# A transformer pair on one core: all q and k products of the attention ahead of v, heads one by one

## What is computed

```python
qkv = (y @ w_qkv[i]).reshape(B, S, 3, N_HEADS, HEAD_DIM)      # 16 heads of 64
...
s_own = jnp.einsum('bhqd,bhqkd->bhqk', qi, k_own) * scale
s_own = s_own + rel_bias[:, rel_bucket(qpos[:, None] - kpos_own[None, :])]
s_own = jnp.where(kpos_own[None, :] <= qpos[:, None], s_own, NEG)
p = jax.nn.softmax(...)
out = jnp.einsum('bhqk,bhkd->bhqd', p, v_own)
...
h = h + o.transpose(0, 2, 1, 3).reshape(B, S, D) @ w_o[i]
```

## Time and profile before

| | |
|---|---|
| median of 3 runs | 975.1 us (972.58 to 975.62) |
| profiled execution | 974.01 us, its span 972.2 us |
| TensorE busy | 926.5 us (95%), 7996 matmuls |
| VectorE busy | 667.2 us (69%) |
| ScalarE busy | 504.9 us (52%) |
| GpSimd busy | 65.2 us (7%) |
| DMA | 177.31 MB, mean 182 GB/s |
| attention's stretch | from 646.93 us (first tile of q2 0) to 765.48 us (end of wo2 3) |

### The profile page before, as it was taken

One profiled execution on the slowest core, in us unless ns is written; L12 is line 12 of the kernel. 1 busy time (PEld: TensorE's weight loads), 2 busy tenths in 40 slices (PEclk: granted clock), 3 DMA queues, 4 the chain that ended last, 5 costly groups with the idle time before them and its releaser, 6 DMA issues.

```text
span 972.2 us, 18558 instructions
## 1 busy us (share of the span) xinstructions
PE 926.5 (95%) x7996; PEld 880.7 (91%) x7996; DVE 667.2 (69%) x1113; ACT 504.9 (52%) x821; POOL 65.2 (7%) x91
## 2 busy tenths in 40 slices
PE   5789999999999999999989999989999999999997
PEld 2588888898899999989989999979998999999997
DVE  3876677557579986778758875465656677777643
ACT  2476666544344556455334444465565566665442
POOL 0100012011000000030000001010000300000001
PEclk9799999999999999999999999999999999999999
DMA  8743222232249985446898775515343345555631
GB/s 321 265 157 127 88 88 91 85 131 88 88 158 359 351 299 219 174 179 253 253 290 318 265 241 186 197 43 197 131 140 108 107 177 196 186 174 166 235 120 44
DMA packets 27681, 177.31 MB, mean 182 GB/s; under 512 B 2864, under 2 KB 5680, under 8 KB 7504
## 3 DMA queue, kind: packets, MB, share of 16 engines
q1 hardware_dynamic: 27600, 176.13, 51.5%
HBM read 174.29 MB, written 1.84 MB: 181 GB/s over the span
## 4 chain that ended last, share of the span: by engine, by line
PE 71%; DVE 12%; ACT 7%; DMA 7%; issue 2%; SPq 0%; DVEq 0%; ACTq 0%
PE ps L1002 38%; PE ps L1008 19%; DVE wl L1696 3%; DMA raw<-in_w_fi_dram 3%; DVE acc L1631 2%; ACT wh L1343 2%; PE ps L1000 2%; DMA raw<-in_ada_dram 1%; DMA raw<-in_w_rest_dram 1%; DVE tmp L1658 1%; PE ps L1046 1%; DMA raw<-in_w_sc_dram 1%; PE ps L1140 1%; PE ps L1054 1%; PE ps L1201 1%
## 5 line engine op out<-in xcount | busy, mean ns | idle before, releaser
L1002 PE MATMUL ps<-HH,wh 128*128 128x256 f32 x1480 | 388.0, 294 | 6.4 <-DVE wl L1696 5.5
L1696 DVE TENSOR_TENSOR wl<-raw,wh 128x1024 fp32r<-128x1024 f32 x265 | 321.4, 1233 | 97.2 <-ACT wh L1343 96.5
L1002 PE MATMUL ps<-HH,wl 128*128 128x256 f32 x1480 | 375.2, 285 | 0.0
L1343 ACT ACTIVATE wh<-raw 128x1024 fp32r<-128x1024 f32 x265 | 272.6, 1040 | 171.8 <-PE ps L1008 105.3
L1002 PEld LDWEIGHTS ps<-HH,wh 128*128 128x128 f32 x1480 | 287.1, 194 | 15.8 <-issue 8.0
L1002 PEld LDWEIGHTS ps<-HH,wl 128*128 128x128 f32 x1480 | 287.1, 194 | 2.1 <-issue 2.1
L1008 PE MATMUL ps<-HL,wh 128*128 128x256 f32 x1480 | 241.5, 286 | 2.6 <-DVE HL L1671 2.2
L1008 PEld LDWEIGHTS ps<-HL,wh 128*128 128x128 f32 x1480 | 207.3, 194 | 3.3 <-DVE HL L1671 2.6
L1002 PE MATMUL ps<-FH,wl 128*128 128x256 f32 x352 | 88.8, 285 | 0.0
L1002 PE MATMUL ps<-FH,wh 128*128 128x256 f32 x352 | 88.1, 279 | 0.0
L1631 DVE SCALAR_TENSOR_TENSOR acc<-raw,silc,acc 128x512 f32<-128x512 f32 x101 | 76.6, 758 | 8.4 <-DMA raw<-in_ada_dram 5.2
(11 more groups left out here) (251 smaller groups left out, 1090.1 us busy)
## 6 DMA issues: line engine op xcount, KB each, us to landing
raw<-in_ada_dram SPq DMA_DIRECT2D x32, 1024.0 KB, 5.3
raw<-in_w_fi_dram SPq DMA_DIRECT2D x22, 1024.0 KB, 4.9
raw<-in_w_up_dram SPq DMA_DIRECT2D x22, 1024.0 KB, 4.8
raw<-in_w_rest_dram SPq DMA_DIRECT2D x20, 1024.0 KB, 4.8
raw<-in_w_in_dram SPq DMA_DIRECT2D x16, 1024.0 KB, 4.8
raw<-in_w_qkv_dram SPq DMA_DIRECT2D x12, 1024.0 KB, 4.8
raw<-in_w_o_dram SPq DMA_DIRECT2D x8, 1024.0 KB, 4.7
raw<-in_w_fo_dram SPq DMA_DIRECT2D x8, 1024.0 KB, 4.9
```

The costliest lines, as they stand in the source:

```text
L1002: e.matmul(o, w[:, k, 128 * t:128 * t + 128], x_hi[:, k0 + k, :], start=first and n + k == 0, **MM)
L1343: e.activation(whl[u % HALF][0][:, 0:n], raw[i % RAW][:, c:c + n], ACT.Copy).then_inc(*a_hi.up(u))
L1696: e.tensor_tensor(wl[:, 0:n], raw[i % RAW][:, c:c + n], wh[:, 0:n].bitcast(F32), ALU.subtract).then_inc(*v_lo.up(u))
```

## The change

- The product list is q2 0, k2 0, q2 1, k2 1, q2 2, k2 2, q2 3, k2 3, then v2 0 to 3.
- A head's task begins h % 4 ticks late. It takes a bank for steps 0 to 4 and gives it back when the transposed weights are copied; for steps 5 to 7 it takes a bank again, the first that is free, once v2 j is made. The extra tick behind a late v2 is gone.
- There are 16 buffers apt in place of 4. QA and KA share their place in SBUF with OHh and OLl.
- wo2 0 and wo2 1 are made in turns: unit 0 of both, then unit 1 of both, then both are closed. While they run, weights are split up to four units beyond the first unit of wo2 0, and no further. A second way, high_first, is written and not used.

```diff
-    QA = sb("QA", [128, 8, T], where=phase)
-    KA = sb("KA", [128, 8, T], where=phase)
-    VA = sb("VA", [128, 2, 1024], where=phase)
+    scores = ExitStack()
+    QA = sb("QA", [128, 8, T], where=scores)
+    KA = sb("KA", [128, 8, T], where=scores)
+    scores.close()
     OH = sb("OHh", [128, 8, T], F32R, where=phase)
     OL = sb("OLl", [128, 8, T], F32R, where=phase)
-    heads = [dict(p=sb(f"ap{i}", [128, 384], where=phase), pt=sb(f"apt{i}", [128, 3, 128], where=phase),
-                  st=sb(f"ast{i}", [128, 8], where=phase), bank=psum[4 + i]) for i in range(4)]
+    VA = sb("VA", [128, 2, 1024], where=phase)
+    PT = [sb(f"apt{i}", [128, 3, 128], where=phase) for i in range(16)]
+    heads = [dict(p=sb(f"ap{i}", [128, 384], where=phase), st=sb(f"ast{i}", [128, 8], where=phase), bank=psum[4 + i])
+             for i in range(4)]
...
-    for kind, j in (("q2", 0), ("k2", 0), ("q2", 1), ("k2", 1), ("v2", 0), ("q2", 2), ("k2", 2), ("v2", 1), ("q2", 3),
-                    ("k2", 3), ("v2", 2), ("v2", 3)):
+    for kind, j in [(kind, j) for j in range(4) for kind in ("q2", "k2")] + [("v2", j) for j in range(4)]:
...
     def attend(h):
+
+        for _ in range(h % 4):
+            yield
         while not open_heads:
             yield
         st, before_attend[h] = open_heads.pop(0)
         for k in range(5):
             emit("att", h, k, st)
+            if k < 4:
+                yield
+        open_heads.append((st, (a_att, ("pt", h))))
+        while ("v2", h // 4) not in made or not open_heads:
             yield
-        if ("v2", h // 4) not in made:
-            while ("v2", h // 4) not in made:
-                yield
-            yield
+        st, before_sum[h] = open_heads.pop(0)
         for k in range(5, 8):
             emit("att", h, k, st)
             if k < 7:
                 yield
-        open_heads.append((st, h))
+        open_heads.append((st, (v_att, ("lo", h))))
         made.add(("oa", h))
...
+    def in_turns(ps):
+
+        last = ps[0]["units"][0] + HALF - 1
+        for n in range(2):
+            for p in ps:
+                run_unit(p, n, last)
+        for p in ps:
+            close_product(p)
...
+    together = {("wo2", 0): (in_turns, ("wo2", 1))}
...
         if k == 0:
             a_ev.wait_ge(e, "plain", named["q2", j]["p"])
             a_ev.wait_ge(e, "plain", named["k2", j]["p"])
-            if before_attend[h] is not None:
-                v_att.wait_ge(e, "lo", before_attend[h])
+            free(e, before_attend[h])
...
         elif k == 5:
             a_ev.wait_ge(e, "plain", named["v2", j]["p"])
             a_att.wait_ge(e, "pt", h)
+            free(e, before_sum[h])
```

More of the change, by code:

```diff
@@ L588, in _program @@
     open_streams = [(st, None) for st in range(STREAMS)]
-    before_head, before_attend = {}, {}
+    before_head, before_attend, before_sum = {}, {}, {}
     def gdn(h):
@@ L769, in after @@
                 drain()
-                misc.give(4, v_att, "lo", dict(open_heads)[0])
+                misc.give(4, *[f[0:1] + f[1] for st, f in open_heads if st == 0][0])
             close(n, p)
@@ L814, in operands_of, with open_banks, run_unit, close_product @@
         return [("parts", src, kt // 2) for kt in kts]
[L816 to L820, removed]
+    def open_banks(p):
+        count = 2 if p["split"] else 1
+        while len(main.order) < count:
+            assert tasks
+            tick()
+        taken = [main.take() for _ in range(count)]
+        p["banks"] = [b for b, _ in taken]
+        p["free"] = [f for _, f in taken]
+    def run_unit(p, n, last=None, part=None):
+        u = p["units"][n]
+        if part != "low":
+            split_up_to(u + HALF - 1 if last is None else last)
             low_of(u)
             if n == 0:
[L823 to L829, removed]
-            until(*operands_of(p, units[u]))
[L831 to L835, removed]
+                open_banks(p)
+            until(*operands_of(p, units[u]))
+        tiles = p["width"] // 128
+        for t in range(tiles):
+            emit("mm", u, t, part)
+            if part == "high" or (n, t) != (len(p["units"]) - 1, tiles - 1):
+                tick()
+    def close_product(p):
         after(p)
         tick()
+    def in_turns(ps):
[5 more added lines that the diff above has]
+            close_product(p)
+    def high_first(ps):
+        last = ps[0]["units"][0] + HALF - 1
+        for p in ps:
+            for n in range(2):
+                run_unit(p, n, last, "high")
+        for p in ps:
+            for n in range(2):
+                run_unit(p, n, last, "low")
+            close_product(p)
+    together = {("wo2", 0): (in_turns, ("wo2", 1))}
     def startup():
@@ L870, in _program @@
     for p in products:
-        run(p)
+        if p["kind"] == "proj" and p["j"] == 0:
+            drain()
+        key = p["kind"], p["j"]
+        if key in together:
+            way, second = together[key]
+            way([p, named[second]])
+        elif key not in [second for _, second in together.values()]:
+            for n in range(len(p["units"])):
+                run_unit(p, n)
+            close_product(p)
     drain()
@@ L980, in sync_engine, with pe_product @@
         d_out.wait_ge(e, "out")
-    def pe_product(e, u, t):
+    def pe_product(e, u, t, part):
         un = units[u]
@@ L991, in pe_product @@
         first = un["at"] == 0 and (p["split"] or t == 0)
-        if first:
+        if first and part != "low":
             free(e, p["free"][b])
         v_lo.wait_ge(e, u)
-        for k in range(kn):
+        for k in range(kn) if part != "low" else ():
             high_of(e, src, k0 + k)
@@ L1002, in pe_product @@
                     e.matmul(o, w[:, k, 128 * t:128 * t + 128], x_hi[:, k0 + k, :], start=first and n + k == 0, **MM)
-        for k in range(kn):
+        for k in range(kn) if part != "high" else ():
             low_part(e, src, k0 + k)
@@ L1008, in pe_product @@
                 ins = e.matmul(o, wh[:, k, 128 * t:128 * t + 128], x_lo[:, k0 + k, :], start=False, **MM)
-        ins.then_inc(*p_mm.up(u, t))
+        if part != "high":
+            ins.then_inc(*p_mm.up(u, t))
     def pe_gdn(e, h, k, st):
@@ L1112, in pe_attend @@
             a_att.wait_ge(e, "pt", h)
+            free(e, before_sum[h])
             vs = slice(64 * h, 64 * h + 64)
-            e.matmul(bank[rows, 0:256], VA[:, 0, vs], A["pt"][:, 0:2, :].rearrange("p a b -> p (a b)"), start=True, **MM)
-            e.matmul(bank[rows, 128:256], VA[:, 1, vs], A["pt"][:, 2, :], start=False, **MM).then_inc(*p_att.up("av", h))
+            e.matmul(bank[rows, 0:256], VA[:, 0, vs], PT[h][:, 0:2, :].rearrange("p a b -> p (a b)"), start=True, **MM)
+            e.matmul(bank[rows, 128:256], VA[:, 1, vs], PT[h][:, 2, :], start=False, **MM).then_inc(*p_att.up("av", h))
     def warm(e, n, b, before):
@@ L1300, in act_attend @@
             p_att.wait_ge(e, "turn", h)
-            e.activation(A["pt"][:, :, :].rearrange("p a b -> p (a b)"), b[:, 0:384], ACT.Copy).then_inc(
+            e.activation(PT[h][:, :, :].rearrange("p a b -> p (a b)"), b[:, 0:384], ACT.Copy).then_inc(
                 *a_att.up("pt", h))
```

## The result

The changed kernel took 987.5 us (median of 4 runs, 981.6 to 990.7) beside 974.7 for the kernel before: 1.0144 of its time, interval 1.0105 to 1.0182. Forecast were 985.7, in a range of 979 to 990: the direction is right and the median 1.8 us off. The profiled execution took 989.2 us, its span 987.4 against 972.2.

The account below looks back on a forecast made before the run. TensorE's queue was taken to bound the kernel. Scores +8.5, waits +2.5, transposes -4.4, values +1.6 and their waits +2.5 made +10.6 us unrounded, 974.0 to 984.6 profiled, a forecast median of 985.7, range 979 to 990.

Parts of the forecast that it names:

- Scores: Attention scores on TensorE: 16 lone heads at 0.98 us, 15.7, against four groups at 1.80, 7.2; +8.5 us.
- Waits ahead of scores: Each group's first head directly behind its k product waits for ScalarE's KA copy: three new waits of 0.82, +2.5 us.
- Transposes: Transposes of the softmax weights on TensorE: 16 x 0.33 = 5.3 us with no wait, against 9.7 before; -4.4 us.
- 4. and 5. Values: Weights times V: lone heads, pairs and fours cost +1.6 us; three waits for VA copies behind v products, +2.5.
- part 6: Output products 0 and 1 in turns, later weight splits held back: covered, at nothing; without that cover 1 to 2 us.
- slower still: Rival: transposes wait as before (+3.4 us) or late weight splits are uncovered (+1 to 2): 987 to 991; chance 0.07.
- Sixteen buffers and the shared place: Buffers for transposed weights, and QA and KA sharing space with OH and OL: no instruction more, nothing on a queue.
- the hidden switch: Rival: 0.23 us of each half-array switch is covered, giving 982.2, or 979.7 if half the waits go; chance 0.14.
- the missing lone price: Rival: a lone head costs its quarter of a group; waits stand against transposes, +0.5, 975.6 us; chance 0.07.
- The faster case: Rival: lone heads cost less than their quarter, the neighbouring product's fill or drain hiding in the other half; 971.5; chance 0.04.

Follow-up runs that it names:

- e11: Changed kernel with heads four together, one tile ahead of first readers, output products one after the other, and heads within a group ordered 0, 2, 1, 3: ratio 1.0016.
- e2: Changed kernel with heads beginning in pairs, the second pair one tick later (h % 4 // 2 ticks): 978.4 us, 1.0035 of the kernel before.
- e1: Changed kernel with output products 0 and 1 made one after the other instead of in turns: 983.0 us, 1.0099 of the kernel before.
- e5: Changed kernel, turns kept, but weights split further ahead during the four half products as buffers come free: 1.0093 of the kernel before's time.
- e4: Kernel before with one edit, heads 0 to 11 beginning h % 4 ticks late so their scores stand alone: 1.0048 of the kernel before's time.
- e6: Changed kernel with one tile let pass ahead of each first reader of a k or v product: 980.4 us, 1.0076 of the kernel before.
- e7: Changed kernel with no head beginning late, four heads side by side directly behind their k product: 975.2 us, 1.0018 of the kernel before.

## Why the prediction was right

1. Scores: a lone head was priced at 0.98 us and took 1.04. The sum of the part, forecast +8.5, is 16 x 1.04 - 4 x 1.80 = +9.4. Both halves of the price stand: streaming alone costs 0.65 more (e11), and a pair costs what a lone head costs (e2). The rest, 1.04 - 0.65 = 0.39, is put down to the switch (forecast 0.33). No run has it by itself: a second pair adds 1.80 - 1.05 = 0.75 to a first, and with that for the streaming it would be 0.29. The Trainium skill's rule that a change of mode drains the array (TensorEngine Tiling (Array Packing), Key Properties) agrees in kind, as each piece costs more than its streaming. The estimate of 0.11 us, worked out in the prediction from a figure of the Trainium skill (TensorE: Matmul & The Clock Gate, Step-by-step), is too small against these 0.29 to 0.39.
2. Waits ahead of scores: one of 0.82, which was there before, and three new ones of 0.78. Forecast 0.82 each. Right.
3. Transposes: 16 x 0.33, no wait. Forecast -4.4, measured the same.
4. and 5. Values: pieces of 0.94 (1.27 less the transposes beside them), 1.00 a pair, 1.69 a group, waits of 0.76. Forecast +4.1, measured: 11.5 - 3 x 0.33 - 6.8 = +3.7.
6. **The step that failed** is part 6, the splits held back: "Covered, at nothing". I counted from the moment when wo2 1 ends, with four units to be split and the first needed 2.88 us later. That is right for ScalarE's high parts. But VectorE's list runs one unit behind ScalarE's: the low part of a unit is put in the list when the next unit's high part is. So five low parts were open (the x5 of VectorE's row), and the first was needed at once. VectorE had the 0.69 us of an add and 1.23 of a low part to do between the end of wo2 1 and the start of wo2 2: 1.92, just the wait in the row. With what it cost the tile around it (2.17 in all) and the low clock (1.5), 3.7 us. The price that I had named for a lost cover, in the sum's part 6 and in the case "slower still", was 1 to 2. Either way of queueing the splits in time (e1, e5) takes the stall away.
7. Sixteen buffers and the shared place: nothing was expected of them, and no wait in TensorE's list names them.

The sum of the pieces, forecast 35.1, is 35.5. With the stall (2.2) and the low clock (1.5) that makes 11.0 + 2.2 + 1.5 = 14.7, against a stretch 14.5 longer.

So the sum of +10.6 was 3.9 us short of the stretch's 14.5 and 3.4 short of the ratio's 14.0, and almost all of that is part 6. That the forecast median came out within 1.8 us (985.7 for 987.5) is in part luck: the medians are only 12.9 us apart, where the ratio has 14.0, the four runs reach over 9 us, and the repetition of the same program has 990.3, just above the range. Of the rivals, the hidden switch and the missing lone price are refuted by the 1.04 of a lone head, in the change and in e4, and by e2 and e11. Of "slower still", the half with the late splits came true, at about twice its price; the half with the waiting transposes did not. The faster case named the right lever, but its mechanism is not there: the transposes' 4.4 us are won in the change and in the runs that keep its order and its lone heads (e1, e5, e6), and the lone heads lose twice that.

## What to carry over

Small pieces put between large ones are not free to be scattered. Here two half-array matmul groups on different halves cost as much as one when they stood side by side (1.05 us against 1.04), and each piece paid some 0.3 to 0.4 us on top of its streaming: look for a group's price, and then for a lone one's, before a schedule spreads a group. When a consumer moves directly behind its producer, count the copy between them for each group, and leave one tile for it; here that took away seven waits of 0.77 us. And when a step of a planner is held back, write out the queue of each engine up to the first thing needed; a list that lags by one turns a cover of 2.9 us into none.

## What was not expected of the hardware

Two float32 heads on different halves took 0.87 us from their first matmul to the next product matmul, one alone 0.85. TensorE's granted clock fell to 0.50 in a stretch behind an idle 1.92 us in one execution of the change (and of e2, e6 and e7), and stayed 1.00 there in another execution of the change's program, where it fell behind the next norm. Which of the two happens, and why the part before the stretch began it anywhere from 644.5 to 650.7 us though its program is the same, stays open; no run tried it.
